# Low parts of a late panel and of two value bands: from GpSimd to the Vector engine, in pieces

## What is computed

```python
h = rmsnorm(x, norm_mix_g[l])
proj = h @ w_in[l]
u = proj[..., :POOL_WIDTH]                       # to the pool mixer
q, k, v = jnp.split(proj[..., POOL_WIDTH:], 3, axis=-1)
a = pool_mixer(u, w_pool[l], pool_scale[l])      # centred means over windows 2, 4, 8, 16
b = neighbourhood_attention(q, k, v, rpb[l])     # each token of the 8 x 64 grid attends to 8 rows x 16 columns
x = x + jnp.concatenate([a, b], axis=-1) @ w_out[l]
```

## Time and profile before

| | |
|---|---|
| median of 3 runs | 1469.0 us (1468.88 to 1469.13) |
| the profiled execution | 1469.04 us |
| its span, first to last instruction | 1467.2 us |
| mean granted TensorE clock | 0.999 of full speed |
| DVE busy | 680.3 us (46%) |
| ScalarE busy | 568.9 us (39%) |
| GpSimd busy | 572.6 us (39%) |

### The profile page before, as it was taken

One profiled execution on the slowest core, in us unless ns is written; L12 is line 12 of the kernel. 1 busy time (PEld: TensorE's weight loads), 2 busy tenths in 40 slices (PEclk: granted clock), 3 DMA queues, 4 the chain that ended last, 5 costly groups with the idle time before them and its releaser, 6 DMA issues.

```text
span 1467.2 us, 19271 instructions
## 1 busy us (share of the span) xinstructions
PE 1453.7 (99%) x7142; PEld 1228.3 (84%) x7142; DVE 680.3 (46%) x1196; ACT 568.9 (39%) x973; POOL 572.6 (39%) x240
## 2 busy tenths in 40 slices
PE   9999999999999999999999999999999999999998
PEld 7888888888888888888888888788889888888886
DVE  6344443533553645454454543848854111224335
ACT  4323232333344434344344432656744223323232
POOL 5424343434533423323223244445133434445442
PEclk9999999999999999999999999999999999999999
DMA  7222221232322222122321553252122232232221
GB/s 281 87 94 86 68 111 64 86 114 86 115 94 90 77 90 75 64 96 75 104 75 57 186 190 112 86 179 87 58 94 93 86 114 86 87 114 86 100 101 58
DMA packets 30093, 147.00 MB, mean 100 GB/s; under 512 B 3040, under 2 KB 7264, under 8 KB 15200
## 3 DMA queue, kind: packets, MB, share of 16 engines
q1 hardware_dynamic: 26352, 132.47, 25.7%
q10 hardware_dynamic: 3696, 13.93, 2.6%
HBM read 139.04 MB, written 7.34 MB: 100 GB/s over the span
## 4 chain that ended last, share of the span: by engine, by line
PE 90%; DVE 5%; ACT 2%; issue 1%; POOL 0%; DMA 0%; ACTq 0%; DVEq 0%
PE bank L407 26%; PE bank L409 25%; PE bank L408 25%; PE bank L887 6%; PE bank L849 3%; PE bank L948 2%; PE bank L866 1%; DVE xlo L1635 1%; PE bank L633 1%; DVE bank L2081 1%; POOL wlo L512 0%; PE bank L753 0%; ACT nt L1524 0%; ACT whi L1147 0%; DVE xres L2134 0%
## 5 line engine op out<-in xcount | busy, mean ns | idle before, releaser
L512 POOL TENSOR_TENSOR wlo<-stage,whi 128x1024 fp32r<-128x1024 f32 (+1 forms) x210 | 525.8, 2526 | 828.7 <-ACT whi L1147 828.7
L1147 ACT ACTIVATE whi<-stage 128x1024 fp32r<-128x1024 f32 (+1 forms) x214 | 216.5, 1061 | 278.5 <-PE bank L409 258.4
L407 PE MATMUL bank<-xhi,whi 128*128 128x512 f32 (+1 forms) x504 | 195.3, 387 | 0.7 <-POOL wlo L512 0.7
L409 PE MATMUL bank<-xhi,wlo 128*128 128x512 f32 (+1 forms) x504 | 194.5, 386 | 0.0
L408 PE MATMUL bank<-xlo,whi 128*128 128x512 f32 (+1 forms) x504 | 194.4, 386 | 0.0
L407 PEld LDWEIGHTS bank<-xhi,whi 128*128 128x128 f32 x504 | 94.7, 188 | 19.7 <-POOL wlo L512 1.1
L1635 DVE TENSOR_TENSOR dr_lo<-hid,dr_hi 128x512 fp32r<-128x512 f32 x32 | 64.5, 2058 | 100.6 <-ACT dr_hi L1150 100.6
L409 PEld LDWEIGHTS bank<-xhi,wlo 128*128 128x128 f32 x504 | 94.7, 188 | 19.3
L408 PEld LDWEIGHTS bank<-xlo,whi 128*128 128x128 f32 x504 | 94.7, 188 | 18.9
L407 PE MATMUL bank<-whi,dr_hi 128*128 128x512 f32 x256 | 99.7, 389 | 0.3 <-DVE dr_lo L1635 0.3
L409 PE MATMUL bank<-whi,dr_lo 128*128 128x512 f32 x256 | 99.6, 389 | 0.0
(11 more groups left out here) (320 smaller groups left out, 3211.9 us busy)
## 6 DMA issues: line engine op xcount, KB each, us to landing
stage<-in_w SPq DMA_DIRECT2D x104, 1024.0 KB, 4.7
stage<-in_w SPq DMA_DIRECT2D x8, 1152.0 KB, 6.1
o_spill<-gt SPq DMA_DIRECT2D x16, 256.0 KB, 6.1
bT<-o_spill SPq DMA_DIRECT2D x4, 1024.0 KB, 8.7
xres<-in_xT ACTq DMA_DIRECT2D x4, 512.0 KB, 7.0
xres<-in_x ACTq DMA_DIRECT2D x1, 2048.0 KB, 9.1
rows<-in_ln ACTq DMA_DIRECT2D x2, 1024.0 KB, 5.1
nv<-v_spill SPq DMA_DIRECT2D x32, 64.0 KB
```

The source lines that it names most:

```text
L407: pe.matmul(dst, a_hi, b_hi, start=start, stop=False)
L409: return pe.matmul(dst, a_lo, b_hi, start=False, stop=stop)
L512: pool.tensor_tensor(lo[:, r], stage[p % 2][:, r], hi[:, r].bitcast(F32), ALU.subtract).then_inc(w_lo, 1)
L1147: act.activation(parts(p)[0][:, r], stage[p % 2][:, r], ACT.Copy).then_inc(w_hi, 1)
```

## The change

POOL no longer makes the low parts of L0+7 and of bands 2 and 3, and makes that of L0+6 in two halves (`split_lo`) instead of four quarters. DVE makes L0+7's low part in quarters in steps 8 to 11, ahead of `turned`; band 2's in two halves in steps 9 and 10, behind `turned`; band 3's in step 12, one half ahead of `turned` and one behind. WO's quarters move from steps 12 to 15 to steps 13 to 16, and `mixed_lo(0)` and `mixed_lo(1)` from steps 13 and 14 to 14 and 15. TensorE's, ScalarE's and SP's code stays.

```diff
@@ gpsimd @@
-            def quarter(p, s):
-
-                (hi, lo), r = parts(p), slice(s * PAN // 4, (s + 1) * PAN // 4)
-                pool.wait_ge(w_hi, 2 * p + s // 2 + 1)
-                last = pool.tensor_tensor(lo[:, r], stage[p % 2][:, r], hi[:, r].bitcast(F32), ALU.subtract)
-                if s % 2:
-                    last.then_inc(w_lo, 1)
-
             def band_lo(hp):
 
                 b = hp % 2
                 pool.wait_ge(l_bhi, hp + 1)
-                if hp >= 2:
-                    pool.wait_ge(e_o, 4 * (hp - 1))
                 pool.tensor_tensor(nv_lo[:, b, :, :], nv[:, b, :, :], nv_hi[:, b, :, :].bitcast(F32), ALU.subtract
                                    ).then_inc(l_blo, 1)
 
             band_lo(0)
-            for m in range(12):
-                if m == 0:
-                    band_lo(1)
-                if m in (2, 3):
-                    quarter(L0 + 6, 2 * (m - 2))
-                    quarter(L0 + 6, 2 * (m - 2) + 1)
-                if m in (6, 7):
-                    quarter(L0 + 7, 2 * (m - 6))
-                    quarter(L0 + 7, 2 * (m - 6) + 1)
-                if m in (7, 11):
-                    band_lo(m // 4 + 1)
+            band_lo(1)
+            split_lo(L0 + 6)
             for p in range(WO + 2, UP + 1):
                 split_lo(p)
@@ vector @@
+            def band_lo(hp, s):
+                b, r = hp % 2, slice(s * NBLK, (s + 1) * NBLK)
+                dve.wait_ge(l_bhi, hp + 1)
+                dve.wait_ge(e_o, 4 * (hp - 1))
+                last = dve.tensor_tensor(nv_lo[:, b, r, :], nv[:, b, r, :], nv_hi[:, b, r, :].bitcast(F32), ALU.subtract)
+                if s:
+                    last.then_inc(l_blo, 1)
+
@@ vector, the loop over i @@
                 if 1 <= i <= NS:
                     normalise(i - 1)
-                if 12 <= i < 16:
-                    row_lo(WO, i - 12)
+                if 8 <= i < 12:
+                    row_lo(L0 + 7, i - 8)
+                if i == 12:
+                    band_lo(3, 0)
+                if 13 <= i < 17:
+                    row_lo(WO, i - 13)
                 if i >= 2:
                     turned(i - 2)
+                if i in (9, 10):
+                    band_lo(2, i - 9)
+                if i == 12:
+                    band_lo(3, 1)
                 if i == 2:
                     keys(1)
...
-                if i in (13, 14):
-                    mixed_lo(i - 13)
+                if i in (14, 15):
+                    mixed_lo(i - 14)
```

## The result

The changed kernel takes 1471.25 us (median of 20 executions, 1470.95 to 1472.01), the kernel before 1468.99 us (20 executions, 1468.81 to 1469.38). The ratio is 1.0016 with a 95% interval of 1.0009 to 1.0022: slower by 2.3 us, clear of noise, and inside the 0.2% that the prediction calls no change. The forecast was 1471.2.

The account below looks back on a forecast made before the run. TensorE is 99% busy, so its waits for DVE's chain decide. DVE's terms sum to +0.67 us; with WO's fourth quarter a step later TensorE loses 2.2: 1469.0 + 2.2 = 1471.2 us, own range 1470.0 to 1471.9.

Parts of the forecast that it names:

- item 1: DVE beside POOL's L0+6: halves instead of quarters hold the CAST and nt pair longer, +1.16 us, bounds 0 to +1.3.
- The bound of 0: Lower bound for L0+6 in halves: no DVE delay if only the total of POOL's time counted (4.9 us against 5.35).
- items 2 and 3: DVE steps 6 and 8: L0+7's quarters leaving POOL shorten the CAST, -0.89 us; band 2 leaving POOL, -0.90 us.
- item 4: DVE steps 9 and 10: band 2's halves stand behind the turned low, outside a pause, +0.60 us each.
- item 5: DVE steps 8 to 12: L0+7's quarters and band 3's first half lie in pauses, 0, bounds 0 and 0.60 us each.
- the rival of pieces that are not hidden: DVE steps 8 to 12: five pieces in pauses each add their full 0.60 us, 1474.2 us; chance 0.13 for over 1471.9.
- item 6: DVE step 12: band 3 leaves POOL, ScalarE sets the pace, second half behind the turned low; step 13 begins +0.10 us.
- WO's fourth quarter (+2.2): TensorE's kk = 1 in early(0): the quarter, moved to step 16, ends at 1062.04, so TensorE starts 2.2 us later.
- The rival of the covered wait: early(0): TensorE is held anyway by L0+7 and keys(3), DVE comes early enough; 1469.7 or 1468.6 us; chance 0.08.
- item 7: DVE: two mixed lows move from steps 13 and 14 to 14 and 15, -0.60 and +0.60 us, 0 behind them.
- The locks as the whole story: Rival: all TensorE waits on DVE in the stage go, nothing new comes; faster, 1466.0 to 1466.6 us; chance 0.03.

Follow-up runs that it names:

- Two experiments: Changed kernel with L0+6 in four quarters on POOL: 1470.2 us; kernel before with L0+6 in two halves on POOL: 1470.18 us.
- the kernel with halves: The kernel before with L0+6's low part in two halves on POOL instead of four quarters, nothing else changed: 1470.18 us.
- Both directions of the experiment: Changed kernel with WO's quarters back in steps 12 to 15: 1470.0 us; kernel before with them in steps 13 to 16: 1470.43 us.
- the first experiment: The changed kernel with WO's quarters back in steps 12 to 15 and nothing else moved: 1470.0 us, ratio 1.0011 to the kernel before.

## Why the prediction was right, point by point

*The lock on L0+6 (item 1, +1.16 us).* Step 4 begins at 1010.70 instead of 1009.33: +1.14 without the offset. Two experiments price it by itself, at 0.9 to 1.05 us (1.36 us above the kernel before of its round against 2.26, or 1470.2 against 1471.25) and at 1.22 us. The bound of 0 is excluded. The rule of the Trainium skill that I weighed there (SBUF — State Buffer, Who interferes with whom: an exclusive lock for the whole instruction) is borne out by the CAST of 2.41 us and by the kernel with halves, where less POOL time made more kernel time. Its other half, that a DVE instruction with two SBUF inputs is held too, no row of the moved pieces shows, since POOL was idle beside all of them (0.68 or 0.69 us each). Rows of the kernel before, in its MLP, do show it. There a low part of the same shape, with both inputs in SBUF, starts 0.52 us behind the start of a POOL half and ends 0.55 us behind its end, with 2.88 us instead of 0.68; the 32 of its kind take 2.06 us in the mean, the eight quarters of WO and WO+1 0.68:

```profile
1301.05 2.85 POOL L512 TENSOR_TENSOR wlo<-stage,whi 128x1024 fp32r<-128x1024 f32 x1
```

```profile
1301.57 2.88 DVE L1635 TENSOR_TENSOR dr_lo<-hid,dr_hi 128x512 fp32r<-128x512 f32 x1
```

*L0+7 and band 2 off POOL (items 2 and 3, -0.89 and -0.90).* Step 7 begins at 1024.71 (1024.22 before), step 9 at 1033.28 (1033.72). Without the offset that is +0.26 and -0.67; the sums were +0.27 and -0.63.

*Band 2's halves behind the turned low (item 4, +1.20) and pieces in pauses at 0 (item 5).* Step 11 begins at 1042.99, +0.53 without the offset, for a sum of +0.57. The pauses of steps 8 to 11 are 0.30 us, so the rival of pieces that are not hidden falls; the kernels with the pieces behind the turned low show what they would have cost. The prediction's remark that two of the eight new pieces are outside pauses miscounts: band 3's second half stands behind the turned low too, and is priced in its item 6.

*Step 12 (item 6, +0.10).* Step 13 begins at 1050.52, +0.65 without the offset, for a sum of +0.67. That ScalarE paces it is seen in the pause of 1.13 us beside the band piece. I used this only to cost the step; that the pause had room for WO's first quarter too, and that the moved quarters were thus for nothing, I worked out only for the experiments.

*WO's fourth quarter (+2.2).* It ends at 1062.28 and TensorE starts at 1062.33, 0.05 us behind instead of 0.14. The matmul is 2.31 us later than before, 2.08 without the offset, and the medians are 2.26 us apart. TensorE's own work ended at 1060.98, 1060.75 without the offset, where the prediction had it at about 1060.7; so the wait is 1.35 us instead of "about 1.5". Both directions of the experiment (1.1 to 1.25 us back, 1.47 us there) confirm the mechanism. No load was late: behind 1062.33 TensorE waits only the 0.6 us for WO+2's low, as before. The rival of the covered wait is what the first experiment builds, and it gave about what that rival named for the kernel with its other waits: 1469.7 summed, 1470.0 measured, with the wait of 0.28 us for the mixed low that item 7 of the prediction ("0 for all behind them") didn't foresee.

*Signs that didn't come as said.* The wait for the nt pair near 1009 was to be over 1 us and is 0.78; the hold shows in two places, 0.35 us for keys at 1007.66 and this one. The wait for L0+7's last quarter was summed at 1.1 us and is 0.90. Neither enters the forecast, since DVE's later wait takes up what TensorE loses there. And the range that the prediction adds up from item 1 at 0 is 1470.0, where its paragraph on the rule says 1470.1.

*The locks as the whole story.* It falls for this change: with its two faults taken out (halves, WO) the time is 1468.8, that is, as before. Yet for the stage it comes near: with all of POOL gone and the pieces in pauses 1465.96 was reached, where the rival named 1466.0 to 1466.6.

*TensorE's clock* stood in no part of the prediction. In the profiled execution of the changed kernel it was at the full level through the stage, but six of its 20 executions took 1471.67 to 1472.01 us at a mean clock of 0.998, against 0.999 in the others, and I can't show where in those the clock was lost.

## What to carry to other kernels

In these traces a GpSimd instruction held a VectorE CAST or TENSOR_SCALAR until it ended (0.42 us alone, 1.30 beside a quarter, 2.41 beside a half). So beside a latency chain on VectorE the length of the single GpSimd instruction counts, not its total: quarters cost 0.9 to 1.2 us less than halves here. Before work is moved onto the engine of the chain, look for its pauses (idle time that ends with another engine) and place each piece ahead of such a wait: 0.68 us of work cost nothing there and 0.60 us on the other side. And when pieces push one another to a later step, follow the last one to its consumer: a panel quarter one step later turned 0.96 us of slack into a wait, of 1.19 us by itself and of 1.35 us in the changed kernel.

## What the runs showed of the hardware that was not expected

TensorE's granted clock can fall to the lower of its two levels in the middle of a kernel that is 99% busy, behind waits that look short. In the kernel with all four quarters behind the turned low TensorE waited 0.62 and 1.33 us between 1042 and 1044.9 us; the clock was then at 1.2 GHz, all through the next wait of 1.63 us, until 1051.7, and each of its five executions was 2.1 us or more above the 1473.0 that the sum gave. The Trainium skill (TensorE: Matmul & The Clock Gate, Part 1: The HAM clock gate) says that a monitor sets this clock by how busy the array has been; the trace agrees in so far as the clock fell at the end of these two waits and rose again after TensorE had been busy without a gap. It doesn't show which executions of one program lose the clock.

With the same 0.63 and 1.35 us of waits and then only 0.90 (three quarters behind) the profiled execution kept it, and three more of the seven were as fast. With L0+6 in quarters and WO in steps 12 to 15, waits of 1.32 and 0.90 us, the profiled execution lost it for some 3.4 us and the fastest of 11 was 1.8 us faster. With L0+6 in quarters alone, with just these two waits, the 11 executions lie within 0.73 us. Its profiled execution has a mean clock of 0.998 too, but it lost it in the first 20 us of the program (0.91 there) and had the full clock in the stage; so a mean clock doesn't tell where it was lost. Which waits lose the clock, and in which executions, stays open. What is shown is that it fell in the stage in two profiled executions, and that a group of the executions with a lower mean clock was slower than the rest of its kernel: by 0.6 to 0.9 us in the changed kernel, 1.2 to 1.6 with WO's quarters back and 1.6 to 2.3 with three quarters behind.
